# Convolution norm and swish of a hybrid decoder step, in two pieces of 512 tokens before the recurrence turns instead of tile by tile in them

## What is computed

```
proj = rmsnorm(x) @ w_in                          # 2816 columns: 1024 convolution, 1792 recurrence
h    = val * sigmoid(gate)                        # 512 convolution channels
out  = causal depthwise convolution(h, width 31)
mu, var over the 512 channels of each token
of   = (out - mu) * rsqrt(var + 1e-5) * ln_g + ln_b
conv_out = silu(of)                               # = of * sigmoid(of)
rwkv_out = RWKV-7 time mixing of the other 1792 columns, a state of 64x64 per head carried from token to token
x = x + concat(conv_out, rwkv_out) @ w_out
x = x + mixture of experts(rmsnorm(x)); final rmsnorm
```

## Time and profile before

| | |
|---|---|
| Median of 3 runs | 1161.65 us (1160.74 to 1165.13) |
| Span of the profiled execution | 1161.0 us; the profile gives no other time of this execution |
| PE busy | 1105.8 us, 95% |
| DVE busy | 671.7 us, 58% |
| ACT busy | 364.6 us, 31% |
| POOL busy | 216.2 us, 19% |

### The profile page before, as it was taken

The page is one execution under the profiler, slowest core; times in us unless marked ns, Lnnn a source line. Parts: engine busy times, 40 slices in busy tenths (PEclk is TensorE's granted clock), DMA queues, the critical chain, the costliest instruction groups (busy, mean ns, idle before and its releaser), DMA issues.

```text
span 1161.0 us, 24215 instructions
## 1 busy us (share of the span) xinstructions
PE 1105.8 (95%) x9392; PEld 668.9 (58%) x9393; DVE 671.7 (58%) x1144; ACT 364.6 (31%) x720; POOL 216.2 (19%) x278
## 2 busy tenths in 40 slices
PE   7999999999999799999999999967999999999987
PEld 5666666666666788999984555534333333333343
DVE  6388999993554788888744232365343443434416
ACT  6000011011322657777641211022223232222324
POOL 4000000010001213323320001002233342332200
PEclk9999999999998899999999999977999999999998
DMA  9211111010000111111242321057999899999739
GB/s 280 69 36 37 37 37 43 20 43 23 1 1 5 16 21 19 19 18 18 52 148 83 109 73 47 35 221 289 394 350 324 306 326 346 416 407 407 297 126 388
DMA packets 97151, 170.92 MB, mean 147 GB/s; under 512 B 44362, under 2 KB 68609, under 8 KB 87779
## 3 DMA queue, kind: packets, MB, share of 16 engines
q1 hardware_dynamic: 89571, 151.79, 36.8%
q0 software_dynamic: 7488, 17.84, 4.4%
HBM read 153.11 MB, written 25.91 MB: 154 GB/s over the span
## 4 chain that ended last, share of the span: by engine, by line
PE 82%; DVE 9%; DMA 5%; ACT 1%; issue 1%; SPq 1%; POOLq 0%; DVEq 0%; ACTq 0%
PE ps L1654 27%; PE ps L2119 14%; PE ps L1969 10%; PE ps L2149 7%; PE ps L1666 6%; PE ps L1687 3%; PE ps L2106 2%; DMA arena<-in_w_exp_up_dram 2%; PE ps L2184 2%; PE ps L1675 1%; DVE arena L2457 1%; PE ps L1999 1%; DMA arena<-in_w_exp_down_dram 1%; DVE arena L2460 1%; DVE arena L2423 1%
## 5 line engine op out<-in xcount | busy, mean ns | idle before, releaser
L1654 PE MATMUL ps<-arena 128*128 128x384 f32 (+1 forms) x1032 | 316.6, 468 | 0.0
L1654 PEld LDWEIGHTS ps<-arena 128*128 128x128 f32 x1032 | 195.3, 190 | 118.0 <-issue 1.9
L2119 PE MATMUL ps<-arena 128*64 x416 | 188.5, 596 | 3.5 <-DVE arena L2874 2.0
L2122 PE MATMUL ps<-arena 128*64 128x512 f32 x416 | 188.5, 596 | 0.0
L2271 DVE SCALAR_TENSOR_TENSOR arena<-arena,cw 128x1024 f32<-128x1024 f32 x240 | 168.2, 777 | 0.4
L2119 PEld LDWEIGHTS ps<-arena 128*64 128x64 f32 x416 | 54.4, 136 | 112.2 <-issue 112.1
L1969 PE MATMUL ps<-arena 128*128 128x512 f32 x256 | 113.1, 596 | 0.0
L1666 PE MATMUL ps<-arena 64*64 64x64 f32 x2960 | 98.2, 219 | 5.9 <-DVE arena L2471 1.7
L2149 PE MATMUL ps<-arena 128*64 x208 | 96.5, 607 | 2.4 <-ACT arena L1411 2.4
L1666 PEld LDWEIGHTS ps<-arena 64*64 64x64 f32 x2960 | 92.3, 135 | 8.6 <-issue 4.7
L2152 PE MATMUL ps<-arena 128*64 128x512 f32 x208 | 96.5, 607 | 0.0
(11 more groups left out here) (365 smaller groups left out, 1536.1 us busy)
## 6 DMA issues: line engine op xcount, KB each, us to landing
arena<-in_w_exp_gate_dram SPq DMA_DIRECT2D x32, 1024.0 KB
arena<-in_w_exp_up_dram SPq DMA_DIRECT2D x32, 1024.0 KB
arena<-in_w_exp_down_dram SPq DMA_DIRECT2D x32, 1024.0 KB, 9.8
arena<-in_w_in_dram SPq DMA_DIRECT2D x22, 512.0 KB, 4.1
arena<-in_x_prompt_dram SPq DMA_DIRECT2D x16, 512.0 KB, 8.3
arena<-y_rows SPq DMA_DIRECT2D x8, 1024.0 KB, 16.0
arena<-in_w_out_dram SPq DMA_DIRECT2D x2, 2048.0 KB
xn_rows<-arena SPq DMA_DIRECT2D x8, 512.0 KB, 2.8
```

What stands on the lines that cost most here:

```text
L1654: ins = pe.matmul(banks(proj_bank(q) + piece)[:, 0:n1 - n0], win[q % 6][:, c, :], xnT[:, c, n0:n1], start=(c == 0), stop=(c == DC - 1))
L2119: pe.matmul(banks(b)[0:HS, :], xgT[b][:, c, 0:HS], wring_gu[:, bass.ds(slot, 1), 0:2, c, :].rearrange("p a w f -> p (a w) f"), start=(c == ...
L2122: ins = pe.matmul(banks(b)[HS:P, :], xgT[b][:, c, HS:P], wgu[b][:, :, c, :], start=(c == 0), stop=(c == DC - 1))
```

## The change

Norm and swish of the 1024 prompt tokens are done in two pieces of 512 tokens. The piece of 64 sample tokens is done late in the turns, where it was before.

- DVE, after projection j = 11: `conv_norm(0)`, which waits for ACT's `conv_root(0)`. After `scaled_a_b(0)` and ahead of turn 0: `conv_norm(1)` and `conv_swish(0)`. In turn 0 after `sum_rk`: `conv_swish(1)`, a wait for it and the memset of `x_flat`, which stood ahead of `scaled_a_b(0)` before and whose space the buffer `conv_gate` now uses.
- ACT: `conv_root(0)` in projection j = 11; after the copies of the last projection, j = 13, `conv_root(1)`, `conv_tanh(0)`, `conv_tanh(1)`, and then `conv_square(2)` as before. Both Tanh results go to one buffer, so the second waits for `conv_swish(0)`. `conv_root(2)` stands in turn 3 beside `gn_root(0)`.
- The turns lose `conv_norm`, `conv_tanh` and `conv_swish` of tiles 0 to 7, and turn 0 loses the common square root.

```
+            def conv_root(p):
+                act.wait_ge(cvar_done, p + 1)
+                act.activation(conv_std(p), conv_std(p), ACT.Sqrt).then_inc(cstd_done, 1)
+            def conv_tanh(p):
+                v = conv_rows(p)
+                act.wait_ge(ln_step, p + 1)
+                g0, b0 = PR["ln_g"][0], PR["ln_b"][0]
+                for c in range(CT):
+                    ins = act.activation(v[:, c, :], v[:, c, :], ACT.Identity, scale=prm[:, g0 + c:g0 + c + 1],
+                                         bias=prm[:, b0 + c:b0 + c + 1])
+                ins.then_inc(ln_sig, 1)
+                act.wait_ge(ln_sig, 2 * p + 1)
+                act.wait_ge(ln_done, p)
+                act.activation(conv_sig(p), v, ACT.Tanh).then_inc(ln_sig, 1)
...
                 if j == 11:
                     conv_square(1)
+                    conv_root(0)
                 if j == ZT - 2:
                     exps(0)
+            conv_root(1)
+            conv_tanh(0)
+            conv_tanh(1)
             conv_square(2)
...
+            def conv_norm(p):
+                dve.wait_ge(cstd_done, p + 1)
+                link(dve.reciprocal(conv_std(p), conv_std(p)))
+                v = conv_rows(p)
+                dve.tensor_tensor(v, v, conv_std(p).unsqueeze(1).broadcast_to(v.shape), ALU.mult).then_inc(ln_step, 1)
+            def conv_swish(p):
+                v = conv_rows(p)
+                dve.wait_ge(ln_sig, 2 * p + 2)
+                dve.scalar_tensor_tensor(out=v, in0=conv_sig(p), scalar=1.0, in1=v, op0=ALU.add, op1=ALU.mult)\
+                    .then_inc(ln_done, 1)
...
                 if j == 11:
                     conv_eps(0)
                     conv_sum(3)
+                    conv_norm(0)
...
             link(dve.tensor_tensor(eye2, ident[:, 0:64], ident[:, 64:128], ALU.add))
-            dve.memset(x_flat, 0.0)
             scaled_a_b(0)
+            conv_norm(1)
+            conv_swish(0)
...
                         ins = dve.tensor_scalar(sum_rk[:, hp, :], headsum[:, :], prm[:, c0:c0 + 1], None, ALU.mult)
                     link(ins)
+                    conv_swish(1)
+                    dve.wait_ge(ln_done, 2)
+                    dve.memset(x_flat, 0.0)
...
-                if j:
-                    conv_norm(j - 1, 0)
-                    conv_norm(j - 1, 1)
                 masked_k(j, mask_ar)
...
                 if j:
                     bonus_v(j - 1)
-                    conv_swish(j - 1)
...
-                if j:
-                    conv_tanh(i)
                 tok_copy(j, 2, ktok, 0)
...
-                    act.wait_ge(cvar_done, len(PIECES))
-                    for v in conv_rstd:
-                        ins = act.activation(v, v, ACT.Sqrt)
-                    ins.then_inc(cstd_done, 1)
```

More of the change, by code:

```diff
@@ L170, in hybrid_decoder_step @@
         w_aa = at(O_EX + N, C)
-        sqt = [at(O_WIN + 8 * C, CT, C), at(O_WIN, CT, C), at(O_WIN + ZW + N + 16 + CT * C, CT, NS)]
+        sqt = [at(O_WIN + 8 * C, CT, C), at(O_WIN, CT, C), at(O_WIN + ZW + N + 16, CT, NS)]
+        conv_gate = at(O_WIN + 8 * C, CT, C)
         csum = at(O_XR + 2 * ZW + N, C)
         assert O_XR + 2 * ZW + N + C <= O_XR + 5 * D - SEQ
-        assert ZW + N + 16 + CT * (C + NS) <= 9 * C
+        assert ZW + N + 16 + CT * NS <= 5 * C
         PIECES = [(n0, min(n0 + C, N)) for n0 in range(0, N, C)]
@@ L406, in hybrid_decoder_step, with conv_rows, conv_std, conv_sig @@
         s_psum, s_sum, s_done, y_psum, y_done = (sem(n) for n in ("s_psum", "s_sum", "s_done", "y_psum", "y_done"))
[L408 to L412, removed]
+        def conv_rows(p):
+            n0, n1 = PIECES[p]
+            return co[:, :, n0:n1]
+        def conv_std(p):
+            n0, n1 = PIECES[p]
+            return conv_rstd[0][:, n0:n1] if n1 <= SEQ else conv_rstd[1]
+        def conv_sig(p):
+            return conv_gate if p < 2 else kb[:, :, 0:NS]
         def tokens_of(i):
@@ L652, in _ @@
             states_stored(1)
-            sp.wait_ge(ln_done, NT)
+            sp.wait_ge(ln_done, len(PIECES))
             for i in range(2, NT):
@@ L1222, in gn_affine @@
                 ins.then_inc(aff_done, 1)
[L1224 to L1235, removed]
             def shift_tail_copy(g):
@@ L1263, in _ @@
                     gn_root(j - 3)
+                if j == 3:
+                    conv_root(2)
                 if j < NT - 1:
@@ L1317, in _ @@
                     act.activation(zs[:, GL0, :], zs[:, GL0, :], ACT.Tanh, scale=0.5).then_inc(gl_tanh, 1)
-                    act.wait_ge(cvar_done, len(PIECES))
-                    for v in conv_rstd:
-                        ins = act.activation(v, v, ACT.Sqrt)
-                    ins.then_inc(cstd_done, 1)
-            conv_tanh(NT - 1)
+            conv_tanh(2)
             gn_root(NT - 3)
@@ L1957, in _ @@
             pe.wait_ge(fin_copied, 1)
-            pe.wait_ge(ln_done, NT)
+            pe.wait_ge(ln_done, len(PIECES))
             pe.wait_ge(gain1_in, 64)
@@ L2472, in new_state @@
                                   ALU.mult).then_inc(s_done, 1)
[L2474 to L2493, removed]
             def gn_centre(i):
@@ L2581, in _ @@
             gn_inverse(i8 - 3)
-            conv_norm(i8 - 1, 0)
-            conv_norm(i8 - 1, 1)
             masked_k(i8, mask_ar8)
@@ L2600, in _ @@
                                   seqmask[:, :, :], ALU.mult).then_inc(a8_done, 1)
-            conv_swish(i8 - 1)
             bonus_v(i8)
-            for k in range(2):
-                conv_norm(i8, k)
+            conv_norm(2)
             rows8 = rowmask[:, :].unsqueeze(2).broadcast_to([P, SB, 64])
@@ L2617, in _ @@
             v_rows(1)
-            conv_swish(i8)
+            conv_swish(2)
             gn_inverse(i8 - 2)
```

## The result

The changed kernel took 1173.38 us (median of 5 runs, 1169.3 to 1175.75), the kernel before 1163.22 us in 5 runs (1160.74 to 1165.13). The ratio is 1.0081 with a 95% interval of 1.0061 to 1.0100, which is 9.4 us (7.1 to 11.6) slower. The forecast was 8.5 us. As a time it was 1170.1 us, added to a median before of 1161.65 from 3 runs; with all 5 runs that median is 1.6 us higher, which is about half of the 3.3 us between 1170.1 and 1173.38. The profiled execution has a span of 1171.6 us, 10.6 over the one before.

A forecast was written before the change was run, and what follows sets the result against it. The prediction took the chain of waits as the bound, with DVE's order setting the time around turn 0's start. Turns 0, boundary +9.95 - 1.47 = +8.5 on span 1161.0, plus 0.65, gives 1170.1 us; range 1164.5 to 1175.

The forecast's parts named there:

- What bounds the turns, and what they lose: Steady turns: the chain of waits decides; DVE loses 2.40 us per full tile, but the gain is taken as 0.
- Piece 0's norm in projection 11: DVE in projection 11: the norm ends at 343.0, inside 8.28 us of idle time, 2.9 us before delaying anything.
- ACT's order behind the last copies: Between the loops: ACT's root waits behind the last copies, so DVE blocks and first_level(0) starts 9.95 us late.
- The three handovers of 0.05 us: Between the loops: three handovers of 0.05 us, counted in first_level(0) starting at 373.1.
- A rule against the rows: ACT's table changes: each costs 1.28 us by the rows, without the 1380 ns drain that the Trainium skill adds.
- Second swish and memset hidden: DVE in turn 0: 3.2 us of work fits 4.47 us of idle time ahead of masked_k, 1.2 us to spare.
- The clock, "I take the same price": PE in turn 0: iclr and second gram at clock 0.50 cost 2.07 + 3.63 us, as before the change.
- one of the prediction's own signs of being wrong: PE behind turn 0: the forecast is wrong if the clock is at 0.50 for longer than before.
- the upper bound: Whole kernel: 8.5 + 1.5 + 0.4 = 10.4 us, with 1.5 for a longer low clock at turn 1's first gram.
- The rival that PE stays at the low level: PE in turn 0: low clock for most of a turn costs 10 us more, 1180 us; 6 in 100.

The follow-up runs named there:

- e3: Changed kernel with norm, affine, Tanh and swish of the 1024 prompt tokens left out altogether: 1162.48 us, ratio 0.9990 against the kernel before.
- e1: Changed kernel with conv_root(1) on ACT moved ahead of the last projection's copies: 1170.24 us, ratio 1.0052 against the kernel before.
- e2: Changed kernel with conv_root(1) and conv_tanh(0) moved ahead of the last projection's copies: 1163.58 us, ratio 1.0008 against the kernel before.
- e8: Changed kernel with one more DVE product of 128x2048 after the second swish in turn 0: 1172.59 us, ratio 1.0072 against the kernel before.
- e9: Changed kernel with one unneeded ACT copy of 128x512 ahead of exps(1) in turn 0: 1171.14 us in one execution.
- e6: Kernel before with 3 unneeded PE matmuls ahead of iclr(1) and 5 behind conv_var(2) in turn 0: 1163.53 us, ratio 1.0000.
- e7: e2 with 3 unneeded PE matmuls ahead of iclr(1) and 5 behind conv_var(2) in turn 0: 1165.01 us, ratio 1.0007 against the kernel before.
- e4: Changed kernel with 17 unneeded PE matmuls ahead of iclr(1) and 9 behind conv_var(2) in turn 0: 1176.96 us, ratio 1.0108 against the kernel before.
- e5: Changed kernel with 11 unneeded PE matmuls ahead of iclr(1) and 5 behind conv_var(2) in turn 0: 1175.62 us, ratio 1.0089 against the kernel before.

## Why the forecast was right, and where it was short

The table sets the steps of the prediction against the two profiled executions. Shifts are start times after minus before. All of them contain the 0.36 us by which the profiled execution was late before it reached the changed place.

| Milestone | Forecast shift | Measured |
|---|---|---|
| Last projection's copies on ACT | 0 | 0.36 (361.25 to 361.61) |
| `first_level(0)` | 9.95 | 10.07 |
| `conv_centre(2)` | 8.5 | 8.50 |
| `masked_k(0)` | 8.5 | 8.43 |
| `gram(1)` | 8.5 | 9.26 |
| `masked_k(1)` | 8.5 | 10.00 |
| `masked_k(7)` | 8.5 | 10.14 |
| End | 8.5 | 10.6 |

- *What bounds the turns, and what they lose.* Right. A window with DVE at 22 of 26 us was no sign of a limit; e3 shows that the whole of the work was hidden.
- *Piece 0's norm in projection 11.* Right: it ended at 343.6 and left 2.67 us of idle time, forecast 2.9. ACT's load for `exps(0)` ran from 349.20 while ACT waited for PE, and cost nothing.
- *ACT's order behind the last copies.* Right, and shown by moving it: e1 took 2 us off, e2 the rest. The chain's terms were met: 2.91 us for the Identity activations (2.93 forecast), 1.91 for the Tanh (1.92), 2.29 for the swish (2.28). The reciprocal took 3.35 us instead of 3.05, within the 0.7 us that it had to spare; DVE then still waited 0.36 us for the Tanh. The three handovers of 0.05 us did not appear. Without the 0.36 us of the table `first_level(0)` moved by 9.7 instead of 9.95 us and `conv_centre(2)` by 8.1; that the table has 8.50 there, as forecast, is luck.
- *A rule against the rows.* The two table loads took 1.28 us each and nothing around them: Identity's end, load 367.78 to 369.06, Tanh 369.07. The drain of 1380 ns that the Trainium skill adds to a load ("ScalarE: Activation LUTs", What ACT_TABLE_LOAD costs) does not appear. By that figure `first_level(0)` would have come 2.8 us later than it did, an estimate for the two loads.
- *Second swish and memset hidden.* Right; 0.89 us to spare against 1.2 forecast, and e8 shows that this was the whole room.
- *The clock, "I take the same price".* Right up to `masked_k(0)`, where `iclr` and the second `gram` took 2.07 and 3.63 us again. Short behind it. Here one of the prediction's own signs of being wrong came true: behind turn 0 the clock was at 0.50 for longer than before. It cost 0.7 us, within the 1.5 us that the upper bound had for it. Windows of PE, first the changed kernel, then the kernel before (stretch, length, busy, granted clock):

```profile
371.00:384.00 13.00, 5.59 (x44) 0.50 0.07 11
384.00:390.80 6.80, 3.82 (x62) 1.00 0.01 2
391.00:401.00 10.00, 5.49 (x42) 0.50 0.19 27
401.00:408.00 7.00, 7.00 (x218) 1.00 0.13 19
```

```profile
370.00:376.50 6.50, 6.50 (x62) 0.50 0.04 10
377.00:383.50 6.50, 2.82 (x30) 1.00 0.02 4
384.00:390.00 6.00, 3.75 (x34) 0.50 0.22 35
```

  In windows of 0.5 us the second low stretch (1.2 GHz) lasts from 390.8 to 401.1, 10.2 us, instead of 383.4 to 390.3, 6.8 us. What counts is the part behind the start of `gram(1)`, 5.6 us instead of 4.0: it takes in more of the matmuls that follow, and from `gram(1)` to `masked_k(1)` it is 13.23 instead of 12.49 us. The other traces go the same way: 4.4 us and 12.68 in e1, 5.8 and 13.28 in e9, 6.1 and 13.41 in e6. The rival that PE stays at the low level for most of a turn had this direction and more than ten times this size.
- *Not in the forecast:* 0.8 us between `masked_k(0)` and `gram(1)`, 11.38 instead of 10.55 us. The sum has no term for it. The timeline above shows it: GpSimd's product starts at 387.70, DVE's block product 0.03 us after it, and DVE's takes 2.10 us; the second block product, at 390.57, takes 1.01. In the kernel before DVE was first, and its two products took 1.02 and 1.25 us:

```profile
379.30 1.02 DVE L2457 TENSOR_TENSOR arena<-arena 64x512 f32<-64x512 f32 x1
...
379.71 1.75 POOL L830 TENSOR_TENSOR arena<-arena 128x512 f32<-128x512 f32 x1 [16.44 <-ACT arena L1098]
...
381.07 1.25 DVE L2457 TENSOR_TENSOR arena<-arena 64x512 f32<-64x512 f32 x1
```

  The two together are 3.11 instead of 2.27 us, which is the 0.8 us.

The 0.36 us ahead of the change and 0.5 us behind the turns are differences of two executions; I have no cause for them. The shift by the changed place itself is 8.1 us, 0.4 less than forecast, and that of what it triggered 1.6, of which the forecast has only the clock's part, as a bound. The two errors have opposite signs, so that 8.5 lies within 1 us of the measured 9.4 is in part luck.

## What to carry to other kernels

Before moving work into an engine's idle time, look at the queue of the engine that it waits for: DVE had 8.5 us free, but its input stood on ACT behind copies that could not run before that idle time was nearly over. Then ask what stands behind the waiting instruction. Taking work out of a loop pays only where a removed step has no wait for another engine right behind it; the idle times in brackets tell that per step, a busy share of 87% does not.

## What the runs showed of the hardware that was not expected

**Two products that start together.** DVE's block product of 64x512 (1.00 and 1.01 us in e8 and e7, where GpSimd does nothing beside it) and GpSimd's product of 128x512 meet in turn 0. Whichever started first kept its speed and the other took longer:

| Run | GpSimd start | GpSimd us | DVE start | DVE us |
|---|---|---|---|---|
| changed | 387.70 | 1.26 | 387.73 | 2.10 |
| e4 | 388.77 | 1.27 | 388.81 | 2.10 |
| e6 | 376.88 | 1.26 | 377.00 | 2.02 |
| before | 379.71 | 1.75 | 379.30 | 1.02 |
| e1 | 386.17 | 1.53 | 385.53 | 1.03 |
| e2 | 379.95 | 1.83 | 379.63 | 1.03 |
| e3 | 379.94 | 1.78 | 379.56 | 1.03 |
| e5 | 386.77 | 2.15 | 386.76 | 1.02 |
| e9 | 387.75 | 1.68 | 387.28 | 1.01 |

The rows of e5 and of e6, the two orders:

```profile
386.76 1.02 DVE L2484 TENSOR_TENSOR arena<-arena 64x512 f32<-64x512 f32 x1
386.77 2.15 POOL L836 TENSOR_TENSOR arena<-arena 128x512 f32<-128x512 f32 x1 [23.08 <-ACT arena L1120]
```

```profile
376.88 1.26 POOL L830 TENSOR_TENSOR arena<-arena 128x512 f32<-128x512 f32 x1 [13.29 <-ACT arena L1098]
```

That one holds the other up is shown by nine alignments; by what, these runs do not tell. The ends give a price: in the three rows with GpSimd first DVE's product ends 0.87 to 0.88 us after GpSimd's, in the six with DVE first GpSimd's ends 1.12 to 1.14 us after DVE's, whatever the starts. It is nearly the whole length of the second, as if the two ran one after the other. The small products of e7 and e8, 0.17 us alone, ended 0.04 to 0.05 us after GpSimd's.

The rule of the first has an exception. GpSimd's next instruction, a copy of 128x8, took 0.19 us in e7 and e8, but 0.98 to 0.99 where it started some 0.33 us behind DVE's second block product, and there DVE's product took 1.25 to 1.27 us although it had started first. Where DVE is on the path and GpSimd is not, it paid here to let GpSimd come second, even by adding work ahead of it (e9, one execution). GpSimd ahead of the large product was no cure: in e7 and e8 it held up a small one instead.

**A faster step that is given back.** In e6 PE's matmuls at full clock brought `masked_k(0)` 2.3 us forward. They also brought the exponentials and so GpSimd's product forward against DVE's chain, which then ran into it: 11.32 instead of 10.55 us up to `gram(1)`. And the clock fell to 0.50 at 384.0, 2.4 us after the last of the added matmuls had ended, and stayed there for 6.8 us as before. `gram(1)`, now earlier, had 6.1 us of that behind its start instead of 4.0; from `gram(1)` to `masked_k(1)` it was 13.41 instead of 12.49 us.
